# The order of wide and narrow matmuls in each column half of a tile

## The reference

```python
h = _rmsnorm(x, attn_norm)
proj = h @ w_in
...
merged = (gates[:, :, 0] * (o_sb @ w_branch[0]) + ...)
x = x + merged @ w_out
u = _causal_dwconv(h2 @ w_up, conv_w, conv_b)
```

## Time and profile before

| | us |
|---|---|
| runs: median (lowest to highest) | 2551.51 (2551.26 to 2552.67) |
| the profiled execution | 2552.63 |
| its span | 2550.8 |
| TensorE matmuls busy | 2496.7 (98%) |
| TensorE weight loads busy | 2165.2 (85%) |
| VectorE busy | 1627.5 (64%) |
| ScalarE busy | 1308.2 (51%) |
| mean DMA traffic | 174 GB/s |

### The profile page before, as it was taken

How to read it: one execution, slowest core, us unless ns; L and a number is a source line. 1 busy time by engine, 2 the same in 40 slices (tenths; PEclk the granted TensorE clock), 3 DMA queues, 4 the chain that set the end, 5 groups by cost and what they waited for, 6 DMA issues and landing times.

```text
span 2550.8 us, 37901 instructions
## 1 busy us (share of the span) xinstructions
PE 2496.7 (98%) x13900; PEld 2165.2 (85%) x13900; DVE 1627.5 (64%) x1971; ACT 1308.2 (51%) x1660; POOL 111.1 (4%) x82
## 2 busy tenths in 40 slices
PE   7999999999999999999999999999999998999998
PEld 6888888889888888888888888888888786889886
DVE  5755654566695676777567756776553856766554
ACT  6545444554445554655355544554353555455553
POOL 3000000000000001000000000000000201100010
PEclk9999999999999999999999999999999999999998
DMA  6664666556565656666566656656555464465453
GB/s 197 192 195 137 190 192 190 148 173 187 164 192 160 209 182 190 187 190 190 185 186 183 187 189 182 185 175 186 172 157 143 142 194 142 118 180 157 141 174 107
DMA packets 515614, 443.38 MB, mean 174 GB/s; under 512 B 27978, under 2 KB 476002, under 8 KB 514979
## 3 DMA queue, kind: packets, MB, share of 16 engines
q1 hardware_dynamic: 515298, 441.53, 58.2%
q0 software_dynamic: 192, 0.18, 0.1%
HBM read 439.54 MB, written 2.10 MB: 173 GB/s over the span
## 4 chain that ended last, share of the span: by engine, by line
PE 92%; DVE 5%; ACT 1%; DMA 1%; issue 1%; SPq 0%; DVEq 0%; ACTq 0%
PE blk L645 86%; DVE weight L1675 1%; DVE arena L1675 1%; PE pa L896 1%; DVE u L1733 1%; PE pa L709 1%; DMA weight_raw<-in_w_mem_kv_dram 0%; PE pa L981 0%; ACT weight L1113 0%; DVE xT L1675 0%; DVE arena L2262 0%; PE pa L700 0%; PE pa L711 0%; PE pa L661 0%; PE pa L999 0%
## 5 line engine op out<-in xcount | busy, mean ns | idle before, releaser
L1675 DVE TENSOR_TENSOR weight<-weight_raw,weight 128x1024 fp32r<-128x1024 f32 (+3 forms) x840 | 1023.5, 1226 | 641.0 <-ACT weight L1113 636.4
L1113 ACT ACTIVATE weight<-weight_raw 128x1024 fp32r<-128x1024 f32 (+3 forms) x840 | 870.6, 1042 | 628.0 <-PE blk L645 593.6
L645 PE MATMUL blk<-u,weight 128*128 128x512 f32 (+1 forms) x5408 | 957.9, 339 | 18.8 <-DVE u L1733 13.8
L645 PEld LDWEIGHTS blk<-u,weight 128*128 128x128 f32 x5408 | 829.1, 190 | 141.3 <-issue 14.7
L645 PE MATMUL blk<-h,weight 128*128 128x512 f32 (+1 forms) x5344 | 924.5, 335 | 3.7 <-DVE h L1675 2.8
L645 PEld LDWEIGHTS blk<-h,weight 128*128 128x128 f32 x5344 | 804.9, 189 | 115.4 <-issue 3.6
L645 PE MATMUL blk<-weight,h 128*128 128x512 f32 (+1 forms) x1296 | 278.9, 376 | 0.0
L645 PEld LDWEIGHTS blk<-weight,h 128*128 128x128 f32 x1296 | 232.2, 188 | 43.1 <-issue 0.3
L645 PE MATMUL blk<-weight,u 128*128 128x512 f32 x768 | 184.9, 400 | 5.7 <-DVE weight L1675 5.7
L645 PEld LDWEIGHTS blk<-weight,u 128*128 128x128 f32 x768 | 146.4, 193 | 39.6 <-DVE weight L1675 7.7
L1675 DVE TENSOR_TENSOR arena<-arena,blk 128x512 f32<-128x512 f32 (+1 forms) x119 | 81.8, 687 | 115.0 <-ACT arena L1163 69.7
(11 more groups left out here) (233 smaller groups left out, 1105.3 us busy)
## 6 DMA issues: line engine op xcount, KB each, us to landing
weight_raw<-in_w_in_dram SPq DMA_DIRECT2D x208, 512.0 KB, 3.7
weight_raw<-in_w_up_dram SPq DMA_DIRECT2D x344, 256.0 KB, 3.2
weight_raw<-in_l_gla_w_in_dram SPq DMA_DIRECT2D x96, 512.0 KB, 3.9
weight_raw<-in_w_down_dram SPq DMA_DIRECT2D x80, 512.0 KB, 3.5
weight_raw<-in_w_branch_dram SPq DMA_DIRECT2D x48, 512.0 KB, 3.7
weight_raw<-in_l_mla_w_in_dram SPq DMA_DIRECT2D x48, 512.0 KB, 3.9
weight_raw<-in_w_mem_kv_dram SPq DMA_DIRECT2D x32, 512.0 KB, 4.5
weight_raw<-in_w_out_dram SPq DMA_DIRECT2D x32, 512.0 KB, 4.3
```

Source lines behind the costliest of these rows:

```text
L645: mm = nc.tensor.matmul(to, lhsT, rhs, start=(kt == 0 and m == 0), stop=(kt == ph.bt - 1 and m == len(ops) - 1))
L1113: nc.scalar.activation(weight_hi[:, r, 0:nk * cols], weight_raw[:, r, 0:nk * cols], ACT.Copy).then_inc(hi_made, 1)
L1675: return nc.vector.tensor_tensor(out_, a, b, op)
```

## The change

In a merged phase the list of a half's matmuls, in which 512 and 256 columns alternate, is reordered: first all those with 512 columns, chunk by chunk, then all those with 256. Nothing else changes.

```diff
--- before.py
+++ after.py
@@ -641,6 +641,8 @@
                         else:
                             o = blk[:, r, c, 0:S * (1 + ph.merged)]
                             ops = [op for k in range(nk) for op in weights_still(o, w[:, :, k, part], x[:, :, k0 + k, :])]
+                            if ph.merged:
+                                ops = ops[0::2] + ops[1::2]
                         for m, (to, lhsT, rhs) in enumerate(ops):
                             mm = nc.tensor.matmul(to, lhsT, rhs, start=(kt == 0 and m == 0),
                                                   stop=(kt == ph.bt - 1 and m == len(ops) - 1))
```

## The result

| | before | changed |
|---|---|---|
| median of 22 runs each, us | 2549.49 | 2552.89 |
| lowest to highest | 2541.97 to 2555.14 | 2549.98 to 2556.85 |
| ratio (95% interval) | | 1.0017 (1.0010 to 1.0023) |
| the profiled execution, us | 2552.63 | 2550.41 |

The change makes the kernel slower by 0.17%, 4.3 us by the ratio and 3.4 by the medians. That is inside the 0.2% that I called no change, but the interval leaves out 1, and I had forecast -1.1 us. The two profiled executions say the opposite (2552.63 and 2550.41): the first lies on the slow side of its kernel's scatter, the second near the quick end of its own. Twenty-two runs tell what one of each can't.

The account below looks back on a forecast made before the run. TensorE's matmuls, busy 98% of the span, were taken as the bound. Slow halves gaining 8.6 us and quick ones losing 7.5 made -1.1 us: 2550.4 us, no change, range 2531 to 2563.

Parts of the forecast that it names:

- TensorE's spacing goes into the time one for one: Projection matmuls (L645), 86% of the last-ending chain: any change in their start-to-start time was to arrive whole in the kernel's time.
- A grouped half takes 1402 ns: Merged phases, four long then four short matmuls: 930 ns after a 256-to-512 border plus 472 ns after a 512-to-256 one.
- The two paces vanish: Merged phases get one pace: `sbqk` 89.7 us (was 88.75, slower), `up1` 179.5 us (was 180.91, quicker).
- The mean half is now 1403 ns: Kernel before, eight matmuls of a tile's column half: 785 slow halves at 1413 ns and 499 quick at 1387.
- Rival (b): Merged phases: long runs pay the whole transient, short ones give nothing back; 1414 ns a half, +14 us, 2564; chance 0.15.
- rival (a): Merged phases: grouping removes the loss, every half takes 1387 ns; -21 us, 2531; chance 0.25.
- A fixed gap by width whoever the neighbour is: Weighed skill rule, columns/2.4 + 2.5 ns: an estimated 1300 ns a half in either order, the change worth nothing.

Follow-up runs that it names:

- kick: Kernel before's alternating order, but each tile in merged phases begins with two 512-column matmuls, then two of 256: 2546.26 us, ratio 0.9993.
- tile8: Changed kernel with grouping over both column halves of a tile, eight 512-column matmuls, then eight of 256: 2545.61 us, ratio 0.9987 to the kernel before.
- two: Changed kernel with groups of two: two 512-column matmuls, two of 256, and again; 2540.81 us, ratio 0.9970, repeated 2543.07 us, 0.9976, to the kernel before.
- snake: As `tile8`, but odd tiles of a block take the 256-column matmuls first: 2539.25 us, ratio 0.9968 to the kernel before.
- kickhalf: Kernel before's alternating order, but each column half begins with two 512-column matmuls, then two of 256: 2558.26 us, one execution.

## Why the prediction was right and wrong

The steps one by one.

- *TensorE's spacing goes into the time one for one, nothing else moves.* Right. The waits stand as in the earlier trace rows, and over five kernels whose mean half is the same in all merged phases the whole follows the half of `up1`. With the changed kernel at 1403.3 ns and 2553 us, `kick` (1398.4), `tile8` (1396.7), `two` (1393.3) and `snake` (1391.6) should take 6, 8, 13 and 15 us less at 1284 halves. Measured: 7, 7, 12 (10 the second time) and 14.
- *A grouped half takes 1402 ns, the sum of two borders.* Right to 1 ns: 1403.3. The transients of the earlier trace rows carry over to runs of four, with shifts inside the half. That costs 1.3 x 1284 = 1.7 us against the forecast.
- *The two paces vanish, `sbqk` loses, `up1` gains.* Right: 89.81 and 179.62 us against 89.7 and 179.5.
- *The mean half is now 1403 ns.* This step failed. It was read from one execution, as "slow: 785 halves; quick: 499", and I took the pace for a property of the program. Up to `up1` four profiles bear that out; behind it eight of the ten merged phases, all but `mlagate0` and `mlagate1`, came out differently in at least one of the four. The mean share of the slow pace over four profiles is 0.49, not 0.61, and the mean half of the kernel before 1386.7 + 0.49 x 26.7 = 1399.8 ns. Against 1403.3 that is +3.5 x 1284 = +4.5 us, and 4.3 are measured. That these agree so closely is partly luck: the four shares run from 0.28 to 0.60, which leaves their mean open by about 0.07, or 2.4 us (an estimate from their scatter). So the sign of the sum hung on the 3 ns by which my baseline was wrong. The same error showed in plain sight: the profiled execution was 1.1 us above the median of three, and it is 3.1 above the median of 22.
- *Rival (b), 1414 ns a half, and rival (a), 1387.* Neither. The changed kernel sits between, and the floor of 1387 is reached only in the quick phases of the alternating order.
- *A fixed gap by width whoever the neighbour is* would have every order here take the same time. Seven orders of the same matmuls (alternating, grouped, `tile8`, `snake`, `two`, `kick`, `kickhalf`) lie between 1387 and 1413 ns a half, so the spacing of these matmuls hangs on their order. The Trainium skill, "TensorE: Matmul & The Clock Gate", "Back-to-back issue gap", gives columns/2.4 + 2.5 ns as the gap of an isolated matmul, and says that in a stream of loads and matmuls both set the spacing. The estimate of 1300 ns a half left that out; no run here times an isolated matmul.

Open: what the state is that a run of short matmuls leaves and the next long ones pay, and why a doubled pair, or at times a break in the stream, changes the pace of what follows. It is not the shape of the long ones' operand, since one row of 512 pays like two rows of 256. The width of the stationary operand takes part, as its load or as the output rows. Not tried were short matmuls of another width, short ones that write to another place in PSUM than the long ones, and loads shortened for the long ones.

## What to carry to other kernels

Where the term to be compared is a few ns on each of thousands of instructions, one profile of the kernel before is not its mean: look whether the same instructions run at different paces in different phases, and if they do, profile it several times before a sum is made against it. Borders between phases with different shapes are ready-made measurements of a new order, as the 1402 ns here. In this stream of two widths runs of four were a poor choice: runs of two (0.9970, 0.9976) and one round for sixteen and sixteen (0.9968) both beat the alternating order and its draw. And a mean over many repeats can hide two values by turns, as in `kick`: look at single tiles before a theory is dropped for missing the mean.

## What the runs showed of the hardware

- A stream of alternating 512- and 256-column `float32r` matmuls, with nothing waiting and a granted clock of 1.00, has two stable paces, 346.7 and 353.3 ns a pair, and keeps one for a hundred microseconds and more. In the four profiles of the kernel before, every change of pace stands at a break in the stream or behind a phase of another shape. In `kick` a doubled pair changed it each time, with no break: tiles of 2777 and 2817 ns by turns.
- The cost of a round of width changes was 3.3 ns for runs of two, 16.6 for four, 20 for eight and for sixteen.
- Loads of 64 columns in place of 128, 134 ns in place of 190 in the records, and 64 output rows in place of 128, changed the pace of a stream (1403 to 1393 ns a half) in which the matmuls seemed to be what binds, since short matmuls start every 120 ns with full loads.
- The same kernel's time also follows the granted clock of its execution: of the changed kernel's 22 runs the two at 0.988 took 2556.2 and 2556.9 us, the four at 0.992 between 2550.0 and 2551.4. So 0.001 of granted clock goes with 1.5 us, as much as many a change is worth.
